# A router with stationary weights on four column tiles of the PE, and the low parts of the mixer tiles formed on DVE

## The reference, cut to what matters

```python
mix = jnp.concatenate([y_pool, y_lru], axis=-1) @ w_out
x = _layer_norm(ALPHA * x + (1.0 + g1[:, None]) * mix, ln1_g, ln1_b)
u2 = x * (1.0 + sc2[:, None]) + sh2[:, None]
y_moe = _hier_moe(u2, w_group, b_group, w_route, b_route, w_gate, w_up, w_down)
x = _layer_norm(ALPHA * x + (1.0 + g2[:, None]) * y_moe, ln2_g, ln2_b)
...
g_logits = (un @ w_group + b_group)     # 4 group logits per token
e_logits = (un @ w_route + b_route)     # 16 expert logits per token
```

## Time and profile before

| | |
|---|---|
| median of 3 runs | 1300.3 us (1299.82 to 1301.27) |
| profiled execution, its own time | 1304.18 us |
| its span in the profile | 1302.2 us |
| PE busy | 1182.5 us, 91% of the span |
| DVE busy | 920.2 us, 71% |
| ACT busy | 500.9 us, 38% |
| POOL busy | 358.5 us, 28% |
| mean granted TensorE clock | 0.956 of full speed |

### The profile page before, as it was taken

How to read it: one execution, slowest core, us unless ns; L and a number is a source line. 1 busy time by engine, 2 the same in 40 slices (tenths; PEclk the granted TensorE clock), 3 DMA queues, 4 the chain that set the end, 5 groups by cost and what they waited for, 6 DMA issues and landing times.

```text
span 1302.2 us, 23073 instructions
## 1 busy us (share of the span) xinstructions
PE 1182.5 (91%) x6683; PEld 963.3 (74%) x6684; DVE 920.2 (71%) x1821; ACT 500.9 (38%) x934; POOL 358.5 (28%) x447
## 2 busy tenths in 40 slices
PE   6889999999999489999997379999999999999495
PEld 2378988988999478888785368888888888888242
DVE  2764988888898689898899875457655745432298
ACT  0525335444533432111111334446544644422175
POOL 1411202212220431211120053344445544332100
PEclk9979999999999699999999589999999999999798
DMA  8814224404413455344333568877998789854673
GB/s 337 293 41 168 66 96 161 141 20 161 161 53 110 150 171 179 130 163 159 130 121 130 182 232 234 236 221 204 302 272 241 211 246 286 250 129 76 211 279 153
DMA packets 112561, 231.44 MB, mean 178 GB/s; under 512 B 11735, under 2 KB 70363, under 8 KB 109419
## 3 DMA queue, kind: packets, MB, share of 16 engines
q1 hardware_dynamic: 98691, 180.50, 39.6%
q0 software_dynamic: 13824, 50.34, 16.5%
HBM read 161.49 MB, written 69.97 MB: 178 GB/s over the span
## 4 chain that ended last, share of the span: by engine, by line
PE 69%; DVE 17%; issue 5%; ACT 4%; DMA 3%; POOL 1%; SPq 1%; DVEq 0%; ACTq 0%; POOLq 0%
PE bank L1599 19%; PE bank L1601 19%; PE bank L1600 19%; PE bank L1552 5%; DMA ada_arena<-in_w_ada 2%; PE bank L1687 2%; DVE ada_arena L1533 2%; PE bank L1573 2%; PE bank L1620 1%; DVE arena L1252 1%; PE bank L1774 1%; DVE ada_arena L1519 1%; DVE st L1255 1%; PE bank L1629 1%; DVE arena L1268 1%
## 5 line engine op out<-in xcount | busy, mean ns | idle before, releaser
L1599 PE MATMUL bank<-parts 128*128 128x256 f32 (+2 forms) x1472 | 513.3, 349 | 38.6 <-ACT arena L775 20.9
L1601 PE MATMUL bank<-parts 128*128 128x256 f32 (+2 forms) x1472 | 496.4, 337 | 0.0
L1600 PE MATMUL bank<-parts 128*128 128x256 f32 (+2 forms) x1472 | 495.9, 337 | 0.0
L1599 PEld LDWEIGHTS bank<-parts 128*128 128x128 f32 x1472 | 283.0, 192 | 82.6 <-ACT arena L775 29.1
L1601 PEld LDWEIGHTS bank<-parts 128*128 128x128 f32 x1472 | 282.7, 192 | 28.6
L1600 PEld LDWEIGHTS bank<-parts 128*128 128x128 f32 x1472 | 283.4, 193 | 25.5
L1552 PE MATMUL bank<-ident,arena 128*128 128x128 f32 (+4 forms) x788 | 116.4, 279 | 14.3 <-DMA arena<-u_d,tok_i 5.8
L1552 PEld LDWEIGHTS bank<-ident,arena 128*128 128x128 f32 (+4 forms) x788 | 94.5, 145 | 39.8 <-issue 9.2
L1442 DVE TENSOR_TENSOR parts<-arena,parts x90 | 105.0, 1221 | 15.9 <-ACT parts L942 14.2
L1454 DVE TENSOR_TENSOR arena<-arena,bank 128x256 f32<-128x256 f32 x48 | 20.1, 419 | 132.3 <-ACT arena L952 131.2
L647 POOL TENSOR_TENSOR arena<-arena 128x256 f32<-128x256 f32 (+1 forms) x36 | 26.1, 728 | 267.9 <-DVE h_last L1181 190.0
(11 more groups left out here) (266 smaller groups left out, 1761.3 us busy)
## 6 DMA issues: line engine op xcount, KB each, us to landing
arena<-in_w_ada SPq DMA_DIRECT2D x16, 1024.0 KB, 8.4
arena<-in_w_gate SPq DMA_DIRECT2D x16, 1024.0 KB, 5.9
arena<-in_w_up SPq DMA_DIRECT2D x16, 1024.0 KB, 12.7
arena<-in_w_down SPq DMA_DIRECT2D x16, 1024.0 KB, 14.5
y_d<-zero SPq DMA_DIRECT2D x17, 512.0 KB, 6.4
ada_arena<-in_w_ada SPq DMA_DIRECT2D x4, 2048.0 KB, 15.4
arena<-in_x_prompt SPq DMA_DIRECT2D x8, 1024.0 KB, 7.8
yT_d<-arena SPq DMA_DIRECT2D x16, 512.0 KB, 4.6
```

What stands on the lines that cost most here:

```text
L1599: pe.matmul(out, x_hi, w_hi, start=start, stop=False)
L1600: pe.matmul(out, x_hi, w_lo, start=False, stop=False)
L1601: return pe.matmul(out, x_lo, w_hi, start=False, stop=stop)
```

## The change: what it does

1. **Router.** Its weights become the stationary operand. `w_rt` is now a tensor of its own, 128 x 8 x 32 with 12 zero columns a k-block, zeroed by POOL at the start. A matmul of k-block 4g + j has a stationary operand of 128x32 and writes the PSUM partitions 32j to 32j + 31 (column tile j); the moving operand is u2T of that k-block, 128x128. Two such groups of four (g = 0, 1) add up in PSUM, which leaves four partial sums, transposed, in bank[6][:, 0:128]. ACT copies them to `rt_sb` (`rt_evac`, between u2T_evac(t - 2) and split_y(t + 2)), and one more matmul (`router_sum`) with `rt_sb` stationary and the 128x20 matrix `pick` moving turns them back and adds the four. `router` moves from (1, 7) to (1, 6); `router_sum` stands behind the whole out_proj of the tile.
2. **Low parts.** y_lo runs on DVE instead of POOL, for all tiles but tile 1. For tile 0 it stands in the last chunk ahead of the recurrence coefficients; for tile t + 2 it stands in ln(t), behind the add of the residual (L1252). `router_out(t - 2)` moves from ahead of ln(t) to behind this y_lo.
3. **Loads of the router's weights.** They move from `load_rows` to the kernel's beginning, ahead of the load of the second chunk of x.
4. **Small things.** DVE forms `pick` at the start (4 instructions of 128x20). Some semaphores are merged (wpool_in into gates_in, late_ok into mod_ok, fin_s_in into fin_in), and tile 1 has its own semaphore for the low part.

```diff
+        w_rt = sb("w_rt", [P, KD, CW])
+        pick = sb("pick", [P, NR])
...
@@ SP
-            sp.wait_ge(S["zero_ok"], 1)
+            sp.wait_ge(S["zero_ok"], 2)
...
+            sp.dma_start(w_rt[:, :, 0:NGR], A["w_group"][0].rearrange("(k p) n -> p k n", p=P)).then_inc(S["rt_in"], 16)
+            sp.dma_start(w_rt[:, :, NGR:NR], A["w_route"][0].rearrange("(k p) n -> p k n", p=P)).then_inc(S["rt_in"], 16)
...
             def load_next(t, b, n=P):
 
-                sp.wait_ge(S["yT_lo_ok"], t + 1)
+                sp.wait_ge(S["yT_lo_ok"], t)
                 load_y(t + 2, b, n)
...
@@ POOL
+            pool.memset(w_rt[:], 0.0).then_inc(S["zero_ok"], 1)
...
-            y_lo(0, 0)
-            y_lo(1, 1)
+            pool.wait_ge(S["yT_hi_ok"], 2)
+            pool.tensor_tensor(yT_lo[1], yTt[1], yT_hi[1].bitcast(F32), ALU.subtract).then_inc(S["yT_lo_1"], 1)
             pool.wait_ge(S["y_stored"], 16 * TPC * (NCH - 1) + 16)
             gate_output(NCH, C, *by_group)
-            y_lo(2, 0)
-            y_lo(3, 1)
-            with pool.Fori(1, NT // 2 - 1) as j:
-                for b in range(2):
-                    y_lo(2 * j + b + 2, b)
-            y_lo(NT - 1, 0, NS)
...
@@ ACT
+            def rt_evac(t, n=P):
+                act.wait_ge(S["rt_part"], t + 1)
+                act.activation(rt_sb[:, 0:n], bank[6][:, 0:n], ACT.Copy).then_inc(S["rt_sb_ok"], 1)
...
                 for b in range(2):
                     u2T_evac(2 * j + b - 2)
+                    rt_evac(2 * j + b - 2)
                     split_y(2 * j + b + 2, b, j + 2)
                     deviation(2 * j + b, b)
...
@@ DVE
+            o.step(dve.tensor_copy(pick[:], ident[:, 0:NR]))
+            for n in range(1, 4):
+                o.step(dve.tensor_tensor(pick[:], pick[:], ident[:, CW * n:CW * n + NR], ALU.add))
...
+            def y_lo(t, b, n=P):
+                dve.wait_ge(S["yT_hi_ok"], t + 1)
+                dve.tensor_tensor(yT_lo[b][:, :, 0:n], yTt[b][:, :, 0:n], yT_hi[b][:, :, 0:n].bitcast(F32),
+                                   ALU.subtract).then_inc(S["yT_lo_ok"], 1)
...
+                if last:
+                    y_lo(0, 0)
                 for j in range(NG):
                     lru_coefficients(i, j, C, a_t, b_t)
...
                 dve.scalar_tensor_tensor(z[b][0:n, :], xres[b][0:n, :], ALPHA, z[b][0:n, :], ALU.mult, ALU.add).then_inc(S["mix_used"], 1)
+                if t + 2 < NT:
+                    y_lo(t + 2, b, P if t + 2 < NT - 1 else NS)
+                if t >= 2:
+                    router_out(t - 2)
                 dve.wait_ge(S["mix_used"], t + 1)
...
-                if t >= 2:
-                    router_out(t - 2)
                 ln(t)
...
@@ PE
-                for k in range(KD):
-                    last = pe.matmul(bank[6][0:n, 0:NR], u2T[:, k, 0:n], w_rt[:, k, :], start=k == 0, stop=k == KD - 1)
-                last.then_inc(S["rt_mm"], 1)
+                for g in range(2):
+                    for j in range(4):
+                        last = pe.matmul(bank[6][CW * j:CW * j + CW, 0:n], w_rt[:, 4 * g + j, :], u2T[:, 4 * g + j, 0:n], start=g == 0, stop=g == 1)
+                last.then_inc(S["rt_part"], 1)
+
+            def router_sum(t, n=P):
+                pe.wait_ge(S["rt_sb_ok"], t + 1)
+                pe.matmul(bank[6][0:n, P:P + NR], rt_sb[:, 0:n], pick[:], start=True, stop=True).then_inc(S["rt_mm"], 1)
...
-                between = {(1, 3): lambda: turn_u2(t - 2, t % 2), (1, 7): lambda: router(t - 2)}
+                between = {(1, 3): lambda: turn_u2(t - 2, t % 2), (1, 6): lambda: router(t - 2)}
...
                 out_proj(t, t % 2, P if t < NT - 1 else NS, between=between)
+                router_sum(t - 2)
```

More of the change, by code:

```diff
@@ L177, in build @@
         row_tiles = [ada_at(off, D) if n < 2 else at(off, D) for n, off in enumerate(ROWS_AT)]
-        w_rt = at(9216, KD, NR)
+        rt_sb = at(9472, P)
         b_rt = at(9376, NR)
@@ L208, in scratch @@
             t = BATCHES[n][1]
-            base, small = (10816, 9396) if n < 3 else (600, 1700)
+            base, small = (10816, 9640) if n < 3 else (600, 1700)
             beat, tie = (at(base + q * 400, 5 * t, EPG * EPG).rearrange("p r (a b) -> p r a b", a=EPG) for q in range(2))
@@ L441, in _ @@
             sp.wait_ge(S["y_stored"], 16 * TPC * (NCH - 2) + 16)
-            sp.wait_ge(S["late_ok"], 1)
+            sp.wait_ge(S["mod_ok"], 2)
             for n in range(2):
@@ L528, in _ @@
             for b in range(2):
-                sp.wait_ge(S["yT_lo_ok"], b + 1)
+                sp.wait_ge(S["yT_lo_1" if b else "yT_lo_ok"], 1)
                 load_y(2 + b, b)
@@ L908, in _ @@
             u2T_evac(NT - 5)
+            rt_evac(NT - 5)
             split_y(NT - 1, 0, NT // 2 + 1, NS)
@@ L911, in _ @@
             u2T_evac(NT - 4)
+            rt_evac(NT - 4)
             deviation(NT - 2, 1)
             u2T_evac(NT - 3)
+            rt_evac(NT - 3)
             deviation(NT - 1, 0, NS)
             u2T_evac(NT - 2)
+            rt_evac(NT - 2)
             for h in range(2):
@@ L919, in _ @@
                                ACT.Copy).then_inc(S["u2T_ok"], 1)
+            rt_evac(NT - 1, NS)
             act.wait_ge(S["w_raw0"], 48)
@@ L1232, in _ @@
             o.wait()
-            dve.memset(spare[0:1, 0:1], 0.0).then_inc(S["late_ok"], 1)
+            dve.memset(spare[0:1, 0:1], 0.0).then_inc(S["mod_ok"], 1)
             chunk(NCH, last=True)
@@ L1508, in _ @@
             y_evac(s, 1, SLOTS // 2 - 1)
-            dve.wait_ge(S["fin_in"], 48)
-            dve.wait_ge(S["fin_s_in"], 16 * DEC_B)
+            dve.wait_ge(S["fin_in"], 48 + 16 * DEC_B)
             def fin_scale(t):
@@ L1706, in sample_mixers @@
             def sample_mixers():
-                pe.wait_ge(S["gates_in"], 64)
-                pe.wait_ge(S["wpool_in"], 16)
+                pe.wait_ge(S["gates_in"], 80)
                 gates(0, range(NG), NS, first=True)
@@ L1813, in _ @@
             for t in range(3, NT):
-                between = {(1, 3): lambda: turn_u2(t - 2, t % 2), (1, 7): lambda: router(t - 2)}
+                between = {(1, 3): lambda: turn_u2(t - 2, t % 2), (1, 6): lambda: router(t - 2)}
                 if t == 3:
                     between[0, 3] = first_router
+                    between[0, 6] = lambda: router_sum(0)
                 if t in COUNT_IN:
@@ L1819, in _ @@
                 out_proj(t, t % 2, P if t < NT - 1 else NS, between=between)
+                router_sum(t - 2)
             turn_u2(NT - 2, 1)
             router(NT - 2)
+            router_sum(NT - 2)
             turn_u2(NT - 1, 0, NS)
             router(NT - 1, NS)
+            router_sum(NT - 1, NS)
             count(3)
```

23 lines of the change are left out of this document (9 added, 14 removed).

## The result

| | before | after |
|---|---|---|
| median of 4 runs each | 1300.43 us | 1285.89 us (1285.22 to 1287.15) |
| ratio to before, 95% interval | | 0.9884 (0.9869 to 0.9900) |
| profiled execution, its span | 1302.2 us | 1284.0 us |
| stage, DVE's tile 0 to tile 16 | 222.98 us | 207.79 us |
| from there to the end of the span | 592.4 us | 593.6 us |

The change makes the kernel 14.5 us faster; 13.5 were predicted, 1286.8 us against 1285.89 measured. The stage, read in one profile of each kernel, gave 15.2.

What follows compares the result with a forecast made beforehand. PE bounds the path to 650.4 us, then DVE to 739. The walk through the tiles moves tile 16 from 709.76 to 696.2, 13.5 us gained, the rest unchanged: 1300.3 - 13.5 = 1286.8 us, range 1282.5 to 1297.5.

Steps and rivals of the forecast that it cites:

- The router: PE, each tile: new router 0.65 us, router_sum 0.21 and a change between products 0.09 against 1.70, saving 0.75.
- 16 pairs cost what 16 cost: Rival on PE: new router costs about 1.70 us as now, plus 0.3 for the sum; gain 3.3, time 1297.0; chance 0.12.
- the Trainium skill's rule: Router on PE: the second group's weight loads would add 0.16 us, saving 0.59 a tile; end 1287.9 instead of 1286.8.
- y_lo on DVE: Low part on DVE, each tile: 1.22 us more, ordinary tile 10.97; all meetings with POOL go.
- the walk: Stage, tile by tile on PE and DVE: tile 16 starts at 696.2 instead of 709.76, 13.5 us gained.
- PE's waits for ACT: Router waiting for ACT's copy: PE waits 0.8 us in tile 9 and 2.5 in tile 14, the latter covered by DVE's lateness.
- dip of the clock: Rival, PE after waits in tiles 9 and 14: each dip costs about 1.7 us; time 1290 to 1293; chance 0.14.
- The beginning: Stage start: PE's first product 1.1 us earlier, from 467.82 to about 466.8; DVE's tile 0 unchanged at 486.78.
- Neither half would give this alone: PE and DVE nearly tied in the stage; with nothing saved on PE, 6.6 us gained instead of 13.5.
- Slower, by y_lo's wait for its tile: Rival on DVE: y_lo in ln(t) waits for split_y(t + 2); gain gone at a mean wait of 1.2 us; chance 0.07.
- The 3.9 us between profile and median of before: Whole kernel: the median lies 3.9 us below the profiled execution of 1304.2, so the forecast started from 1300.3.

Runs made afterwards that it cites:

- experiment 8: Changed kernel with the two groups of the router's matmuls issued twice, 16 more pairs of load and matmul a tile: median 1290.34 us, ratio 0.9912.
- Experiment 7: Also called `ylo_late`: changed kernel with y_lo on DVE moved behind the variance, ahead of the wait for ACT's root: median 1287.31 us, ratio 0.9886.
- ylo_twice: Changed kernel with each low part of ln(t) formed twice on DVE: median 1301.15 us, ratio 0.9991.
- gated_tile2_again: Second run of the kernel `gated_tile2`, unchanged: median 1283.45 us, ratio 0.9863.
- experiment 2: Changed kernel with the low parts of tiles 2 to 16 back on POOL, new router kept: median 1288.37 us, where 1294 to 1301 was expected.
- gated_third: Third run of the changed kernel with low parts of tiles 2 to 16 on POOL, each waiting for DVE's residual add: median 1285.18 us, ratio 0.9864.
- gated_tile2: Changed kernel with low parts on POOL, each waiting for DVE's residual add, but tile 2's formed by DVE: median 1282.00 us, ratio 0.9846.

## Why the prediction was right

**The router.** 0.65 + 0.21 + 0.09 against 1.70, saving 0.75: measured 0.77 a tile. The new router is 0.57 us and not 0.65, the sum 0.14 + 0.08 at the change of operand and not 0.30; against that stands 0.09 at the router's front (0.32 us from the product ahead to its first matmul, where products follow at 0.23), which I had left out. The rival "16 pairs cost what 16 cost" is refuted by the 0.57 us itself and by experiment 8. By the Trainium skill's rule (TensorE: Matmul & The Clock Gate, "Part 3: Packing small matmuls") that a weight load overlaps only where the row groups differ 0.59 would have been saved; the measured 0.77 speaks against it for these four column tiles, and so does experiment 8, where a group costs no more with its loads than streaming alone was estimated at.

**y_lo on DVE.** Forecast 1.22 a tile, measured 10.77 - 9.75 = 1.02: neighbouring instructions overlap, so y_lo of 1.22 us busy moves the next by 1.13 (585.52 to 586.65 in tile 8), and the one behind the residual add starts 1.14 us after it where it was 1.26. This term was mis-sized, and so was the wait for ACT in tile 9, below. With 1.1 and 0.77 the walk gives 14.2 us; without the wait for ACT in tile 9 as well it gives 15.0, measured 15.2, against the 13.5 on record.

**The walk.** Less the 4.1 us by which its tile 0 came earlier, the profile of after has tile 5 at 544.0 (predicted 543.6), tile 8 at 587.2 (587.1), tile 10 at 609.5 (609.9), tile 13 at 653.8 (655.0), tile 16 at 694.6 (696.2). Up to tile 10, where PE takes part, it agrees to 0.5 us; behind it 1.2 us more come from DVE's shorter tiles.

**PE's waits for ACT.** 0.8 us in tile 9 and 2.5 in tile 14 were forecast, none and 0.92 appeared. From the start of ln(t - 1) to the router that waits for the copy the walk had 7.0 us; the wait in tile 14 ends after 656.36 - 649.63 = 6.7. Only the wait of tile 14 was covered by DVE's lateness as said. That of tile 9 stood on the walk's path, as PE sets the start of tile 10, and it cost the forecast the 0.8 us above. Experiment 7 removes the wait of tile 14 and gains nothing by it. No dip of the clock came behind either place; the granted clock is 1.00 from 470 to 690 us.

**The beginning.** In `ylo_twice` and `gated_tile2_again`, which share the slow start of before, PE's first product stands at 466.86 and 466.44 against 467.82: 1.0 and 1.4 us earlier, 1.1 predicted. DVE's tile 0 is 0.65 and 1.2 us earlier, where I had it unchanged: another term set at nothing too early, if a small one.

**"Neither half would give this alone".** True in the letter: 7.1 and 10.9 of 15.2. But for the router alone the expectation of experiment 2 was too low a gain, since it let every meeting with POOL count; the meetings of the tiles that PE sets cost nothing.

**Slower, by y_lo's wait for its tile.** No y_lo waited. The loads came in time, and most tiles wait for PE first. The 3.9 us between profile and median of before I took off without knowing why. Of its late start 1.8 us are there by 63 us and 3.3 by 95, in part at a granted clock of 0.50. That the forecast for the median came within 1 us is no proof of the walk: the median is known to about 2 us, the beginning gave about 1 us that the sum lacks, and the stretch behind the stage, whose time varies by 2 us between profiles of one kernel, was taken as unchanged.

## What to carry to other kernels

Where two engines are nearly tied, price each tile on both and walk through the tiles; a saving on one engine alone gives part. By the stage the parts don't add up (10.9 and 7.1 gave 15.2), though the medians can't show that. Before moving work off an engine because it collides with another, look which instruction it collides with: the same work started one instruction later cost a quarter of what it costs on the other engine. Then look at the first tiles, where a later start of a shared operand makes PE pause.

## What the hardware showed that was not expected

- **POOL beside DVE.** A POOL subtraction of 128x1024 ran beside bn_stats, the aggregation and a 128x1 reciprocal without holding them up, and held up a scalar_tensor_tensor of 128x1024 until it was done (1.54 us for 0.46 us of common time, 3.29 for a common start, 1.23 to 1.27 alone).
- **The clock after a pause.** In tile 2 PE paused 1.92, 2.04 and 2.46 us in three profiles, and in each the granted clock fell to 0.50 one to two us after the pause, for about 3 us; after six pauses of 0.40 to 0.80 us there it stayed at 1.00. But ahead of the stage's first product PE paused 2.46 to 4.06 us in all fourteen profiles, and the clock fell behind seven of them only, the shortest and the longest among these: the length of the pause doesn't settle it. Nor does it in the kernel before, where the clock fell to 0.50 behind a pause of only 0.59 us in tile 9. A fall at the first place costs little: the stage takes 207.8 us with it and 207.3 without in the changed kernel, 205.7 and 205.0 in `gated_tile2`. PE then has little or no pause in tile 2. Without it PE comes to tile 2 early, and in `ylo_late`, `gated_third` and `ylo_twice` it paused long and the clock fell; in the first two PE sets the pace there, so that it counted.
- **One program, two starts.** The same 16 products at 29 us took from 1.92 to 3.64 us in different executions. They follow a wait for a DMA, and its length goes with their time: in five profiles with a wait of 3.46 to 3.75 us they took 3.52 to 3.64, in eight with 1.80 to 2.20 they took 1.92 to 3.03; only the profile of before has 3.64 behind a wait of 1.68. The four profiled executions with 3.64 took 2.2 to 3.9 us more than the median of their own set. A single profile can be off by this much.
- **Small stationary operands.** A further pair of weight load and 128-column matmul on four column tiles costs 0.028 us (experiment 8), a pair with a full 128x128 stationary operand and 20 moving columns 0.106.
